# The order of the experts in a mixture-of-experts loop: a computed table of places, and one written out

## The reference, cut to what matters

```python
logits = (xt @ w_router + b_router).astype(jnp.float32)
top_vals, top_idx = lax.top_k(logits, TOP_K)
...
def expert_block(args):
    xb, e = args
    gate = xb @ w_gate[e] + b_gate[e]
    up = xb @ w_up[e] + b_up[e]
    gate = jnp.minimum(gate, SWIGLU_LIMIT)
    up = jnp.clip(up, -SWIGLU_LIMIT, SWIGLU_LIMIT)
    glu = gate * jax.nn.sigmoid(SWIGLU_ALPHA * gate)
    return (glu * (up + 1.0)) @ w_down[e] + b_down[e]
```

## Time and profile before

| what | before |
|---|---|
| median of 3 runs | 2930.44 us (2929.05 to 2930.51) |
| span of the profiled execution | 2927.8 us |
| TensorE busy | 2770.9 us, 95% |
| first end of a block in the loop, D1 | 1781.9 us |
| end of D49, the last pass of the loop | 2897.5 us |

### The profile page before, as it was taken

How to read it: one execution, slowest core, us unless ns; L and a number is a source line. 1 busy time by engine, 2 the same in 40 slices (tenths; PEclk the granted TensorE clock), 3 DMA queues, 4 the chain that set the end, 5 groups by cost and what they waited for, 6 DMA issues and landing times.

```text
span 2927.8 us, 38771 instructions
## 1 busy us (share of the span) xinstructions
PE 2770.9 (95%) x12668; PEld 1659.7 (57%) x12668; DVE 1525.6 (52%) x3062; ACT 956.4 (33%) x1806; POOL 115.4 (4%) x171
## 2 busy tenths in 40 slices
PE   7899999999999999999999989999998999998998
PEld 5676678888778677888877763332322332321332
DVE  5984778875673554333375544343333433432435
ACT  4734342222563434222333322222222232222222
POOL 0000000000000003000020000000000000000002
PEclk9999999999999999999999979999999999999999
DMA  8271246864323035342323069789899879899898
GB/s 267 72 218 41 88 130 186 236 187 125 99 87 87 15 87 168 98 115 83 97 73 107 1 258 410 289 327 409 321 410 410 322 298 410 319 410 410 349 381 318
DMA packets 398912, 638.18 MB, mean 218 GB/s; under 512 B 34576, under 2 KB 284560, under 8 KB 398816
## 3 DMA queue, kind: packets, MB, share of 16 engines
q1 hardware_dynamic: 381024, 590.80, 56.1%
q0 software_dynamic: 9376, 31.14, 3.1%
q10 hardware_dynamic: 8416, 14.95, 1.5%
HBM read 610.79 MB, written 26.02 MB: 218 GB/s over the span
## 4 chain that ended last, share of the span: by engine, by line
PE 72%; DMA 10%; SPq 5%; DVE 5%; ACT 4%; issue 3%; POOL 0%; POOLq 0%; ACTq 0%; DVEq 0%
PE bank L2625 23%; PE bank L196 14%; PE bank L198 13%; PE bank L197 13%; DMA ring<-w_down 6%; SPq L2430 4%; DMA ring<-w_gate 2%; PE bank L1084 1%; PE bank L1125 1%; PE bank L1085 1%; DMA pairs<-w_ada 1%; DVE WLO L167 1%; PE bank L2619 1%; ACT WHI L157 1%; PE bank L1118 0%
## 5 line engine op out<-in xcount | busy, mean ns | idle before, releaser
L2625 PE MATMUL bank<-ring,xT 128*64 128x512 f32 x3200 | 728.5, 597 | 25.2 <-DMA ring<-w_up 12.4
L196 PE MATMUL bank<-HH,WHI 128*128 128x512 f32 x1344 | 540.4, 402 | 33.0 <-DVE WLO L167 15.7
L197 PE MATMUL bank<-HL,WHI 128*128 128x512 f32 x1344 | 530.3, 395 | 0.0
L198 PE MATMUL bank<-HH,WLO 128*128 128x512 f32 x1344 | 530.0, 394 | 0.0
L2625 PEld LDWEIGHTS bank<-ring,xT 128*64 128x64 f32 x3200 | 220.1, 137 | 496.8 <-issue 363.1
L2625 PE MATMUL bank<-ring,hT 128*64 128x512 f32 x1600 | 370.0, 598 | 26.4 <-DMA ring<-w_down 26.1
L167 DVE TENSOR_TENSOR WLO<-RAW,WHI 128x2048 fp32r<-128x2048 f32 (+1 forms) x132 | 281.6, 2134 | 105.2 <-ACT WHI L157 105.0
L196 PEld LDWEIGHTS bank<-HH,WHI 128*128 128x128 f32 x1344 | 257.0, 191 | 97.0 <-DVE WLO L167 21.5
L157 ACT ACTIVATE WHI<-RAW 128x2048 fp32r<-128x2048 f32 (+1 forms) x132 | 234.6, 1777 | 166.6 <-PE bank L198 134.6
L197 PEld LDWEIGHTS bank<-HL,WHI 128*128 128x128 f32 x1344 | 256.8, 191 | 55.6 <-issue 2.9
L198 PEld LDWEIGHTS bank<-HH,WLO 128*128 128x128 f32 x1344 | 256.5, 191 | 54.5
(11 more groups left out here) (466 smaller groups left out, 2777.9 us busy)
## 6 DMA issues: line engine op xcount, KB each, us to landing
ring<-w_gate SPq DMA_DIRECT2D x256, 512.0 KB, 9.4
ring<-w_up SPq DMA_DIRECT2D x256, 512.0 KB, 15.0
ring<-w_down SPq DMA_DIRECT2D x256, 512.0 KB, 16.0
RAW<-w_ffn_in SPq DMA_DIRECT2D x88, 512.0 KB, 5.2
RAW<-w_ada SPq DMA_DIRECT2D x40, 1024.0 KB, 5.2
RAW<-w_in SPq DMA_DIRECT2D x37, 1024.0 KB, 5.7
RAW<-w_ffn_out SPq DMA_DIRECT2D x32, 704.0 KB, 4.7
expert_results<-ysb ACTq DMA_DIRECT2D x98, 128.0 KB, 5.5
```

The costliest lines, as they stand in the source:

```text
L196: pe.matmul(out, lhi, rhi, start=start, stop=False)
L197: pe.matmul(out, lhi, rlo, start=False, stop=False)
L198: return pe.matmul(out, llo, rhi, start=False, stop=stop)
L2625: ins = pe.matmul(out[halves(h), :], xT[:, k % 4, halves(k // 4)], m["ring"][:, c, h * 512:(h + 1) * 512], start=False, stop=k == KD - 1)
```

## The change

The formula for the places goes, and a list takes its place: entry p of the list is the rank of the expert at place p + 1. Nothing else differs.

```diff
-PLACE_STEP, FIRST_PLACE = 12, 3
+RANKS_BY_PLACE = (23, 12, 25, 1, 17, 14, 7, 16, 0, 29, 15, 8, 30, 6, 21, 4, 27, 10, 22, 3, 19, 11, 18, 5, 28, 9, 20, 2, 24, 13, 26)
...
-    n = EXPERTS - 1
     place = np.zeros(EXPERTS)
-    for k in range(n):
-        place[1 + k] = 1 + (FIRST_PLACE + PLACE_STEP * k) % n
+    for p, rank in enumerate(RANKS_BY_PLACE):
+        place[1 + rank] = 1 + p
```

## The result

The kernel with the written-out list takes 2934.58 us (median of 19 runs, 2931.59 to 2936.82). The kernel before, run beside it, takes 2930.14 us (19 runs, 2928.06 to 2931.48). The ratio is 1.0015, with a 95% interval of 1.0009 to 1.0021: 4.4 us more, small but clear of the noise of so many runs. The forecast was 2935.3 us, 4.9 more than before. The profiled execution has a span of 2933.0 us against 2927.8.

What follows compares the result with a forecast made beforehand. The prediction took two alternating bounds, TensorE's expert matmuls and the DMA loads into the ring. The middle gives 27.3 us and the end takes 32.2: 2930.44 + 4.9 = 2935.3 us, range 2928 to 2941.

Steps and rivals of the forecast that it cites:

- Prices of a run: Stalls for singles between larger experts: 8.10 us for two after 3 or 4 blocks, 10.72 each further, 1.49 after 2 blocks.
- No stall in 3 1 2 1 3: In the middle, the singles between experts of 3, 2 and 3 blocks were to cost 0 us.
- 2.62 us in hand: One single after an expert of 3 or 4 blocks leaves 2.62 us spare, covering a following pair's 1.49.
- Where the engines rest: DMA engines stand still in the third and fourth block of an expert, because the slots are still in use.
- The middle gives 27.3 us: Stalls from D2 to D48 fall from 91.24 to 63.91 us, so D48 ends 27.3 us earlier.
- The end gives back 32.2: After D48, remaining ring loads, D50's eight loads and 16 gathers share the DMA engines; the end takes 32.2 us.
- Equal halves, D50 last: At the end, ring and gathers share DMA equally; gathers finish first, D50's weights land last at T + 61.1; chance 0.53.
- 21.8 us behind D50: Picks, dg matmuls, last sums, norm and store after D50's end take 21.8 us, unchanged.
- The second rival, the fallen clock: Starved TensorE's clock falls at the end, costing 2.5 us more: +7.4, or 2937.8 us; chance 0.20.
- the likeliest case: At the end, D50's weights land last, behind the gathers: 2935.3 us, own range 2933 to 2940; chance 0.53.
- The sum: Whole kernel: the middle gives 27.3 us, the end takes 32.2, so 4.9 us more.

Runs made afterwards that it cites:

- the seven experiments with this run: The runs on the kernel after with edits at its end only; medians from 2923.08 to 2934.78 us.
- experiment 3: The order before with only the head changed: its third expert (2 blocks) exchanged with a single of the first run of four; 2931.37 us, ratio 1.0007.
- experiment 4: Head and end of the order before, between them all large experts side by side, then 17 singles in one run; 3021.51 us, ratio 1.0315.
- experiment 9: After, with SyncE's waits for the gathers behind D50's loads and VectorE's first four sums of gathered rows behind its block 50 work; 2925.47 us, ratio 0.9985.
- experiment 5: After, with SyncE's two waits that let POOL gather moved behind the issue of D50's loads; 2933.49 us, ratio 1.001 to the kernel before.
- Experiments 1 to 3: After with a 2-block expert last again, 2929.53 us; before with a single last, 2935.01 us; before with four singles at the head, 2931.37 us.
- edits 5 and 9: On after: gather waits behind D50's loads, 2933.49 us alone; VectorE's first four sums behind block 50's work, 2934.78 us alone; both, 2925.47 us.

## Why the prediction was right, step by step

- *Prices of a run.* They carried over. The three k = 2 stalls after a large expert were 7.51, 8.13 and, at D37, 2603.03 - 2573.74 - 21.26 = 8.03; 8.10 was the price. Further singles cost 10.74. The five k = 1 stalls behind a 2-block expert were 1.47 to 1.54, with 1.49 as price.
- *No stall in 3 1 2 1 3.* Slightly off: D32 shows 2488.70 - 2466.77 - 21.26 = 0.67, and the seven experiments with this run 0.88 to 1.52, where -2.62 + 1.49 = -1.13 had been said. The step "2.62 us in hand" was wrong: only a part of it reaches the next pair. In the pass of the first block of the 2-block expert of a run 3 1 2 the windows of the trace leave the DMA engines 1.2 us of rest in after, and 2.1 in experiment 3, where 2.4 us more of stall were measured than expected. The 2-block experts of the order before show no such rest. That the ring is full there once more, and the time in hand is spent waiting for slots, fits this but wasn't tested by itself. The 3.6 us of experiment 4 stand behind a chain of 2-block experts, and no run takes them apart.
- *Where the engines rest.* The prediction put the rest into the third and fourth block of an expert. In the trace of before it is 12 to 13 us in the pass of the second block, 19 in that of the third of a 4-block expert, and 2 to 3 in that of the last, because in the last block the slots come free. The sums don't use the place.
- *The middle gives 27.3 us.* It gave 26.9.
- *The end gives back 32.2.* From D48 to the end it takes 82.3 us after and 51.6 before: 30.7. The term that was mis-sized is the gathers: 1.42 us each (370 GB/s) had been taken, and with the ring's loads beside them everything moves at 410, 1.28 each, 2.2 us less for 16. The last landing is at T + 58.9 (T is the end of D48), and T + 61.1 had been said. Gathers are not a slower kind of transfer. In experiment 9 they are alone on the DMA engines in this window, with several queued:

```profile
2900.00:2908.00 8.00, 5.60 (x26) 2.25 (x22) 5.66 (x5) 0.00 (x0) 3.49 (x3) 0.97 1.03 410
```

In before, POOL's issues from the fifth to the tenth lie 1.6 to 2.2 us apart instead of 1.25, and the first ten landed 6.0 to 6.3 us behind their issue (7.5 to 19.3 in after): they hardly queued. Why POOL was slower there is open.
- *Equal halves, D50 last.* As said: 2.55 us for a chunk and for a gathered piece. By the Trainium skill, "DMA: Bandwidth & Descriptors", Queues, rings and completion order, an engine goes round-robin over the queues that have work; here the trace agrees, with one piece of either queue every 2.55 us. D49 came at T + 39.6 and not at about T + 44. Without gathers it is T + 28.4 and not T + 29.4 (experiment 5), and the sharing began not at T + 12 but at T + 16.8, when the gathers' bytes began to move, 4 us behind the first issue. From there D49's last chunk needed twice the 10.4 us that it needs alone. The gathers had also been said to be through well ahead of the ring. They were not: from T + 16.8 on, 16 gathers stood against 16 loads, and the last of each landed within 1 us of each other. D50 ended at T + 60.0; T + 62.0 had been said.
- *21.8 us behind D50.* 22.35. The second rival, the fallen clock, came true beside the likeliest case, and somewhat smaller: the granted clock is 0.50 in the last window of after. D50's last chunk took 1.97 us instead of 1.08, and the first 12 matmuls behind it 3.70 instead of 2.85, so together 1.7 us and not 2.5. Its condition, gathers that take nearly all of the DMA engines, wasn't needed: half was enough.
- *The sum.* -26.9 + 30.7 is +3.8 from D1 on (1149.8 - 1145.9 = 3.9), and the medians differ by 4.4. The misses partly cancel: D50's last weights were 3.1 us earlier than said, and the lower clock gave back 1.7 of it. That the sum is within 0.5 us is in part luck; that the middle's gain is paid back at the end, and how, is not.

The one thing that the prediction didn't see is how it hangs together. It counted stall by stall, and the gain of the middle and the loss of the end looked like two mechanisms. Experiments 1 to 3 show one: 31 experts' weights have to come through at 410 GB/s, the DMA engines rest almost only inside the experts of 3 and 4 blocks, and in all these orders they rest 119 to 122 us. What an order saves at one place it pays at another. D48 came 26.9 us earlier because 24 loads fewer stood ahead of it, and these, 24 x 1.28 = 30.7 us, then stood behind it. The rest is 4 us: TensorE's last passes don't cover these loads, and D50's weights come last, with TensorE's 22 us still behind them.

## What to carry to other kernels

When the loads are a queue that stays behind, count the bytes and the time in which the queue is forced to rest, not the stalls: an order that doesn't change the forced rest changes nothing in the middle. Put last what needs no load of its own, because there the transfers that only the end has (here 16 gathers) take half of the bandwidth from it. And when two queues share the DMA engines at the end, let the one go first that has the longer chain of work behind it, and look for the wait that this creates on the other engines: edits 5 and 9 were worth 1 and 0 us alone and 9 us together.

## What the runs showed of the hardware that was not expected

- With loads from SyncE's queue and gathers from POOL's in flight together the core moved 410 GB/s for some 40 us, the same as with the loads alone (2852 to 2862 us) or the gathers alone (experiment 9). Each queue had a 512 KB transfer land every 2.55 us.
- TensorE's granted clock fell although it was never idle for long. Between chunks that came 2.56 us apart it stood still for at most 1.5 us, and the mean clock of 2880 to 2908 us was 0.68, with 0.50 (1.2 GHz) from 2900 to 2912 us. In the single runs, where a chunk comes every 1.3 us, it stayed at 1.00.
- Moving 12 matmuls out of the way saved less than their time, because the ones behind them then met the lower clock: 4.77 us for what had taken 2.74.
